# Prompt attention of a two-path decoder step: mask, maxima and inverse sums of a round taken once over four PSUM banks

## The chip, the cores and the metric

The kernel runs on one core of one Trainium2 chip. The metric is the device time of one execution in microseconds (us), lower is better. Three runs of the kernel before took 1689.76, 1691.87 and 1692.32 us, so its median is 1691.87 us.

## The reference, cut to what matters

The whole step is a two-layer decoder trunk (gMLP mixing, attention with three branches, two SwiGLU layers) over 512 prompt tokens and 8 x 4 sample tokens, all in fp32. The change touches only the prompt's attention in two of its branches: the selected blocks (with 8 blocks and a top 16, all of the causal past is selected) and the sliding window of 512 (again all of the causal past). For both, per head and query:

```python
s = einsum(q, k) * HEAD_DIM ** -0.5          # 512 keys at most, 16 heads in 4 groups, head size 64
s = where(mask, s, -inf)                     # causal
m = max(s, axis=-1)                          # of a row; 0 if not finite
e = where(mask, exp(s - m), 0)
p = e / maximum(sum(e), 1e-30)
o = gate_cmp * o_cmp + gate_slc * (p_slc @ v_slc) + gate_win * (p_win @ v_win)
```

## The kernel before, in words

Each engine runs its own program in order; they meet at semaphores. The long stages around the one that is changed are weight products (line 573 and line 601), which take most of the span. The stage of the prompt's attention runs over PAIRS = 32 rounds. Round u takes one query tile of 128 rows (`pair`: tile 3 first, eight rounds for each tile, so rounds 0 to 7 have 512 keys, 8 to 15 have 384, 16 to 23 have 256 and 24 to 31 have 128) and two heads, which lie in partitions 0 to 63 and 64 to 127 of the same query column. A round has two halves v = 2u and 2u + 1: branch 0 (selected) and branch 1 (window). The names of the steps in order:

- TensorE `scores(v)` (line 946): q times k for both heads, into PSUM banks 0 and 1 for branch 0, banks 2 and 3 for branch 1. It waits until the exponentials of the same branch in the round before have read these banks (`a_ex`). Both scores of a round are issued back to back.
- VectorE `maxima(v)` (lines 1986 to 1988): adds the causal mask to the diagonal tile of two banks, takes the row maxima over two banks, and makes the bias of the exponentials; then raises `a_mx`.
- ScalarE `exps(v)` (line 1455): two exponentials with their row sums, PSUM to the SBUF tile PB; raises `a_ex`.
- VectorE `inverse_sums(v)` (lines 1993 and 1994): one over the sums; raises `a_f`.
- GpSimd (line 2123): scales both halves of PB by the inverse sums and the branch's gate.
- TensorE `turn_probs(v)` (line 960): transposes PB into banks 5 to 7, three buffers that rotate over v and head. The second head of half 2u - 1 takes the bank that ScalarE must first have read for half 2u - 2.
- ScalarE (line 1469) and VectorE (line 2002) `probs_turned(v)`: copy the transposes of one head each into PTs.
- TensorE `weigh(v)` (lines 973 and 978): probabilities times values; ScalarE `heads_out` (line 1461) stores the sum of the three branches.

The order in which each engine does these in round u is written out by hand:

- TensorE: scores(2u), scores(2u+1), weigh(2u-4), weigh(2u-3), turn_probs(2u-2), turn_probs(2u-1).
- ScalarE: exps(2u), heads_out(u-2), probs_turned(2u-2), exps(2u+1), probs_turned(2u-1).
- VectorE before: inverse_sums(2u-1), maxima(2u), maxima(2u+1), probs_turned(2u-2), inverse_sums(2u), probs_turned(2u-1).

In round 0 VectorE also does `block_sums(3)` for the compressed branch between the two maxima, which GpSimd and then TensorE's `block_turn` (line 936) need before round 1. The cache rows of the last samples are loaded by a queue that waits for the last weigh of this stage, and the sample stage (line 1015 and on) begins on TensorE behind it.

Of the kernel before, what the change touches and what calls it, by code (L numbers as in the profile page):

```python
# [9 lines left out]
ALU = mybir.AluOpType  # L10
ACT = mybir.ActivationFunctionType
AX = mybir.AxisListType

P = 128
# [19 lines left out]
SCALE = HD ** -0.5  # L34
NEG = -1e30
FLOOR = -1e29
# [12 lines left out]
A_P1 = A_P0 + 2 * ACTB  # L49
# [8 lines left out]
C_BONE, C_CAUS, C_CMP = 0, 128, 256  # L58
# [91 lines left out]
def build_program(nc, x_prompt, x_sample, cache_kv_cmp, cache_kv_slc, state_kv_win, page_table,  # L150
# [9 lines left out]
    def at(name, addr, shape, dt=F32):  # L160
        return nc.alloc_sbuf_tensor_at(name, shape, dt, offset=addr)

    def sem(name):
        return ctx.enter_context(nc.semaphore(name))
# [28 lines left out]
    late = at("late", A_X, [P, C_LATE])  # L193
# [3 lines left out]
    gates = at("gates", A_X + C_LATE * 4 + 768, [P, TT, 3 * NH])  # L197
# [40 lines left out]
    PB = at("PB", A_P0, [P, 4, 2, PAST])  # L238
# [2 lines left out]
    vcz = at("vcz", A_P0 + 16384, [P, NG, R, HD])  # L241
    PTs = [at(f"PTs{j}", a, [P, 2, PAST]) for j, a in enumerate((A_SG, A_P1 + 17408, A_P1 + 29696))]
    PTc = kvtok[:, 0:QT, 0:NG * P]
    hst = at("hst", A_P1 + 34816, [P, 4, 8])
    cstat = at("cstat", A_P1 + 34944, [P, 2, 4, NH])
    PD = at("PD", A_P0, [P, 2 * (PAST + TD) + 32])
    PTd = at("PTd", A_P0 + 4608, [P, 8, P])
# [11 lines left out]
    PS = ctx.enter_context(nc.psum_tensor("PS", [P, 8, 512], F32))  # L259
# [41 lines left out]
    a_s, a_mx, a_ex, a_f, a_p = sem("scores_done"), sem("row_maxima"), sem("exponentials"), sem("inverse_sums"), sem("probs_scaled")  # L301
# [42 lines left out]
    def pair(u):  # L344

        return QT - 1 - u // (NH // 2), u % (NH // 2) // R, u % R

    def head(p, g2, r):
        return (2 * p + g2) * R + r
# [802 lines left out]
    def _(act):  # L1152
# [132 lines left out]
        for t in range(TT):  # L1285
            m = P if t < QT else TD
            act.activation(flat[0:m, t * D:(t + 1) * D], xtok[0:m, t, :], ACT.Square,
                           accum_out=stats[0:m, C_MS + t:C_MS + t + 1]).then_inc(sq_ready, 1)
# [87 lines left out]
        for t in range(TT):  # L1376
            m = P if t < QT else TD
            ins = act.activation(gates[0:m, t, :], PS[0:m, 0, t * 48:t * 48 + 48], ACT.Sigmoid,
                                 scale=stats[0:m, C_RS + t:C_RS + t + 1])
# [68 lines left out]
        def exps(v):  # L1448
            qt, br = pair(v // 2)[0], v % 2
            W = (qt + 1) * P  # L1450
            act.wait_ge(a_mx, v + 1)
            if v >= 4:
                act.wait_ge(a_pt, 2 * v - 6)
            for g2 in range(2):
                act.activation(PB[:, v % 4, g2, 0:W], PS[:, 2 * br + g2, 0:W], ACT.Exp, bias=hst[:, v % 4, 2 + g2:3 + g2],  # L1455
                               scale=SCALE, accum_out=hst[:, v % 4, 4 + g2:5 + g2]).then_inc(a_ex, 1)

        def heads_out(u):
            qt, p, r = pair(u)
# [11 lines left out]
        for u in range(PAIRS + 2):  # L1471
            if u < PAIRS:
                exps(2 * u)
            if u == 0:
                act.wait_ge(s_out, OUTS)
                for j in range(QT):
                    act.wait_ge(b_pt, j + 1)
                    act.activation(PTc[:, QT - 1 - j, :], PS[:, 4 + j, :], ACT.Copy).then_inc(b_pe, 1)
            if u >= 2:
                heads_out(u - 2)  # L1480
            if 1 <= u <= PAIRS:
                probs_turned(2 * u - 2)
            if u < PAIRS:
                exps(2 * u + 1)
            if 1 <= u <= PAIRS:
                probs_turned(2 * u - 1)
            if u == 1:
                fill()
                act.wait_ge(z_q, 1)
            if 3 <= u < 7:  # L1490
                sample_queries(2 * u - 6)
                sample_queries(2 * u - 5)
# [57 lines left out]
    def _(dve):  # L1550
        link = Link(dve, dstep)
# [347 lines left out]
        def block_sums(j):  # L1899
            f = cstat[:, 1, j, :]  # L1900
            dve.wait_ge(b_ex, j + 1)
            link(dve.tensor_reduce(f, ecmp[j][:, :, 0:NCMP], AX.X, ALU.add))
            link(dve.tensor_scalar(f, f, 1e-30, None, ALU.max))
            link(dve.reciprocal(f, f))
            g = gates[:, QT - 1 - j, :].rearrange("p (h b) -> p h b", b=NBR)[:, :, 0]
            dve.tensor_tensor(f, f, g, ALU.mult).then_inc(b_f, 1)
# [38 lines left out]
        def cmp_norm(y):  # L1945
            c = y // 2
            n = 2 * NCMP * CHUNK_N[c]
            k, r = chunk(kcr, y).rearrange("p s a m -> p (s a m)"), krs[:, 0:n]
            dve.wait_ge(n_sum, c + 1)
            dve.tensor_scalar(r, PS[:, 7, 0:n], 1.0 / HD, EPS, ALU.mult, ALU.add).then_inc(n_ms, 1)  # L1950
            dve.wait_ge(c_sq, c + 1)
            link(dve.reciprocal(r, r))
            dve.scalar_tensor_tensor(out=k, in0=k, scalar=knc[:, :], in1=r, op0=ALU.mult, op1=ALU.mult).then_inc(n_done, 1)
# [6 lines left out]
        for y in range(CUNITS):  # L1960
# [16 lines left out]
            cmp_join(y)  # L1977
            if y >= 1 and y % 2 == 1:
                cmp_norm(y - 1)
        def maxima(v):  # L1980
            qt, br = pair(v // 2)[0], v % 2
            st = hst[:, v % 4, :]
            S2 = PS[:, 2 * br:2 * br + 2, :]
            d = S2[:, :, qt * P:qt * P + P]
            dve.wait_ge(a_s, v + 1)
            link(dve.tensor_tensor(d, d, late[:, C_CAUS:C_CAUS + P].unsqueeze(1).to_broadcast([P, 2, P]), ALU.add))
            link(dve.tensor_reduce(st[:, 0:2], S2[:, :, 0:(qt + 1) * P], AX.X, ALU.max))  # L1987
            dve.tensor_scalar(st[:, 2:4], st[:, 0:2], FLOOR, -SCALE, ALU.max, ALU.mult).then_inc(a_mx, 1)

        def inverse_sums(v):  # L1990
            f = hst[:, v % 4, 6:8]
            dve.wait_ge(a_ex, 2 * v + 2)
            link(dve.tensor_scalar(f, hst[:, v % 4, 4:6], 1e-30, None, ALU.max))
            dve.reciprocal(f, f).then_inc(a_f, 1)

        def probs_turned(v):
            u = v // 2
            W = (pair(u)[0] + 1) * P
            dve.wait_ge(a_pt, 2 * v + 2)
            if v >= 3:  # L2000
                dve.wait_ge(a_o, v - 2)
            dve.tensor_copy(PTs[v % 3][:, 1, 0:W], PS[:, 5 + (2 * v + 1) % 3, 0:W]).then_inc(a_ptd, 1)

        for u in range(PAIRS + 1):
            if u >= 1:
                inverse_sums(2 * u - 1)
            if u < PAIRS:
                maxima(2 * u)
                if u == 0:
                    block_sums(QT - 1)  # L2010
                maxima(2 * u + 1)
            if u >= 1:
                probs_turned(2 * u - 2)
            if u < PAIRS:
                inverse_sums(2 * u)
            if u >= 1:
                probs_turned(2 * u - 1)

        W = PAST + TD
# [65 lines left out]
    @block.gpsimd  # L2085
    def _(pool):
        def few_tokens(few, g):
            pool.tensor_tensor(few[:, :, :], hT[:, :, TP:T], gains[:, g:g + KT].unsqueeze(2).to_broadcast([P, KT, TD]),
                               ALU.mult).then_inc(f_ready, 1)

        pool.wait_ge(xn_ready, KT)
        few_tokens(few_v, 0)
        pool.wait_ge(xn_ready, 3 * KT)
        few_tokens(few_k, 32)
        few_tokens(few_q, 8)
        pool.wait_ge(g_d, 1)
        pool.wait_ge(c_ss, 1)
        for j in range(QT):
            pool.memset(ecmp[j][:, :, :], 0.0).then_inc(z_set, 1)
        pool.wait_ge(n_done, 1)  # L2100
        pool.memset(kbd, 0.0).then_inc(b_kd, 1)
        pool.wait_ge(b_kd, 1)
        for p in range(2):
            for g2 in range(2):
                rows = slice(64 * g2, 64 * g2 + 64)
                pool.tensor_copy(kbd[rows, p, 32 * g2:32 * g2 + NCMP], kcr[rows, 0, p, :]).then_inc(b_kd, 1)
        for j in range(QT):
            for n, ready, op, done in ((0, b_mx, ALU.subtract, b_sh), (1, b_f, ALU.mult, b_p)):
                if j == QT - 1 and n == 0:
                    pool.wait_ge(t_eva, (TK + TQ) // 2 + TQ)  # L2110
                    pool.memset(vcz[:, :, :, :], 0.0).then_inc(z_set, 1)
                    pool.wait_ge(c_mm, CUNITS)
                    pool.memset(Qbd[:, :, :, :, :], 0.0).then_inc(z_q, 1)
                e = ecmp[j][:, :, 0:NCMP]
                pool.wait_ge(ready, j + 1)
                pool.tensor_tensor(e, e, cstat[:, n, j, :].unsqueeze(2).to_broadcast([P, NH, NCMP]), op).then_inc(done, 1)
        for v in range(HALVES):
            (qt, p, r), br = pair(v // 2), v % 2
            pool.wait_ge(a_f, v + 1)
            for g2 in range(2):  # L2120
                x = PB[:, v % 4, g2, 0:(qt + 1) * P]
                c = 3 * head(p, g2, r) + 1 + br
                pool.tensor_scalar(x, x, hst[:, v % 4, 6 + g2:7 + g2], gates[:, qt, c:c + 1], ALU.mult, ALU.mult).then_inc(a_p, 1)

    ctx.close()

# [29 lines left out]
```

## Time and profile before

| what | value |
|---|---|
| time of the profiled execution | 1692.25 us |
| its span | 1690.4 us |
| median of three runs | 1691.87 us |
| TensorE matmul busy | 1621.9 us, 96% |
| VectorE busy | 867.5 us, 51% |
| ScalarE busy | 558.1 us, 33% |
| GpSimd busy | 93.0 us, 6% |
| mean granted TensorE clock | 0.987 |
| line 573 in the chain that ended last | 61% |
| line 601 in that chain | 13% |
| lines 960, 973 and 946 (this stage) | 2%, 1% and 1% |

Busy time is the time in which an instruction of the engine runs; idle time before an instruction is put down to what released it. The chain that ended last is followed back from the last instruction to what it waited for. In the timelines, consecutive instructions of one line are merged, with their number behind an x: `x8` of line 946 are the scores of both halves of a round, since each fp32 product runs as two passes.

### The profile page before, as it was taken

How to read it: one execution, taken by the hardware profiler on the slowest of the kernel's cores; microseconds unless marked ns; L12 is line 12 of the kernel's file. 1: busy time of each engine (PE TensorE's matmuls, PEld its weight loads, DVE VectorE, ACT ScalarE, POOL GpSimd, SP SyncE). 2: the span in 40 equal slices, each digit the busy share in tenths (PEclk: the TensorE clock that was granted, in tenths of full speed). 3: DMA queues.
4: the chain of work that ended last, by engine and by line, in shares of the span. 5: the costliest groups of instructions: out<-in, count | busy, mean ns of one | idle time of the engine just before them, and what ended most of it. 6: DMA issues, size and time to landing. Idle time of an engine off the chain costs nothing.

```text
span 1690.4 us, 31723 instructions
## 1 busy us (share of the span) xinstructions
PE 1621.9 (96%) x12994; PEld 1503.0 (89%) x12994; DVE 867.5 (51%) x1417; ACT 558.1 (33%) x965; POOL 93.0 (6%) x154
## 2 busy tenths in 40 slices
PE   8999999999999999999998889988889999999998
PEld 7988999999999999999997547655589999999998
DVE  4227754355444444354185779995456444524433
ACT  6334321232212121144344557664343221212111
POOL 0000000000000000000000034551000000000000
PEclk9998999999999999999999989999999999999999
DMA  4247212323232323122244240004532323232211
GB/s 157 75 164 247 75 57 75 105 87 100 75 94 80 100 75 99 63 87 76 78 143 138 76 143 8 2 2 150 150 96 80 96 79 99 75 100 75 100 57 71
DMA packets 134701, 156.70 MB, mean 93 GB/s; under 512 B 11226, under 2 KB 119058, under 8 KB 134194
## 3 DMA queue, kind: packets, MB, share of 16 engines
q1 hardware_dynamic: 134530, 155.42, 28.9%
q8 instruction: 63, 1.03, 0.3%
q14 instruction: 28, 0.23, 0.0%
q10 hardware_dynamic: 80, 0.02, 0.0%
HBM read 149.58 MB, written 14.16 MB: 97 GB/s over the span
## 4 chain that ended last, share of the span: by engine, by line
PE 90%; DVE 5%; ACT 3%; issue 1%; DMA 1%; POOL 0%; DVEq 0%; POOLq 0%; SPq 0%; ACTq 0%
PE PS L573 61%; PE PS L601 13%; PE PS L960 2%; PE PS L891 2%; PE PS L973 1%; PE PS L946 1%; PE PS L608 1%; PE PS L1062 1%; PE PS L751 1%; ACT PB L1455 1%; PE PS L1028 1%; PE PS L864 1%; DVE hst L1987 1%; PE PS L614 1%; PE PS L1015 1%
## 5 line engine op out<-in xcount | busy, mean ns | idle before, releaser
L573 PE MATMUL PS<-act0h,wh 128*128 128x272 f32 x1664 | 346.1, 289 | 1.6 <-DVE sg L1760 1.6
L573 PE MATMUL PS<-act0l,wh 128*128 128x272 f32 x1664 | 344.6, 288 | 0.0
L573 PE MATMUL PS<-act0h,wl 128*128 128x272 f32 x1664 | 344.5, 288 | 0.0
L1158 ACT ACTIVATE wh<-raw 128x2048 fp32r<-128x2048 f32 x106 | 203.0, 1915 | 407.5 <-PE PS L573 407.5
L1556 DVE TENSOR_TENSOR wl<-raw,wh 128x2048 fp32r<-128x2048 f32 x106 | 243.1, 2293 | 176.3 <-ACT wh L1158 176.3
L573 PEld LDWEIGHTS PS<-act0h,wh 128*128 128x128 f32 x1664 | 260.7, 189 | 2.2 <-issue 1.7
L573 PEld LDWEIGHTS PS<-act0l,wh 128*128 128x128 f32 x1664 | 260.5, 188 | 0.0
L573 PEld LDWEIGHTS PS<-act0h,wl 128*128 128x128 f32 x1664 | 260.4, 188 | 0.0
L1589 DVE TENSOR_TENSOR hT<-PS,hT 128x544 f32 (+1 forms) x72 | 52.1, 724 | 214.5 <-PE PS L573 214.2
L601 PE MATMUL PS<-wh,act0h 128*128 128x256 f32 x448 | 130.0, 290 | 0.0
L601 PE MATMUL PS<-wh,act0l 128*128 128x256 f32 x448 | 126.2, 282 | 0.0
L601 PE MATMUL PS<-wl,act0h 128*128 128x256 f32 x448 | 126.2, 282 | 0.0
L573 PE MATMUL PS<-act1h,wh 128*128 128x272 f32 x576 | 119.1, 288 | 0.0
L573 PE MATMUL PS<-act1l,wh 128*128 128x272 f32 x576 | 119.0, 287 | 0.0
L573 PE MATMUL PS<-act1h,wl 128*128 128x272 f32 x576 | 118.9, 287 | 0.0
L573 PE MATMUL PS<-act2h,wh 128*128 128x272 f32 x512 | 106.8, 290 | 5.9 <-DVE act2l L2072 5.9
L573 PE MATMUL PS<-act2l,wh 128*128 128x272 f32 x512 | 106.3, 289 | 0.0
L573 PE MATMUL PS<-act2h,wl 128*128 128x272 f32 x512 | 106.2, 289 | 0.0
L1604 DVE TENSOR_TENSOR sg<-PS,rsb 128x544 f32<-128x544 f32 x44 | 31.7, 724 | 140.5 <-PE PS L573 140.1
L1227 ACT ACTIVATE sg<-sg 128x544 f32<-128x544 f32 x44 | 28.9, 659 | 204.8 <-DVE sg L1604 204.8
L601 PEld LDWEIGHTS PS<-wh,act0h 128*128 128x128 f32 x448 | 84.7, 189 | 10.8 <-issue 10.7
L573 PEld LDWEIGHTS PS<-act1h,wh 128*128 128x128 f32 x576 | 89.8, 188 | 0.0
(300 smaller groups left out, 2507.2 us busy)
## 6 DMA issues: line engine op xcount, KB each, us to landing
raw<-in_ffn_w_gate SPq DMA_DIRECT2D x44, 512.0 KB
raw<-in_ffn_w_up SPq DMA_DIRECT2D x44, 512.0 KB
raw<-in_a_w_in SPq DMA_DIRECT2D x32, 512.0 KB
raw<-in_ffn_w_down SPq DMA_DIRECT2D x32, 512.0 KB
raw<-in_a_w_out SPq DMA_DIRECT2D x16, 512.0 KB
crows<-in_cache_kv_cmp SPq DMA_DIRECT2D x32, 256.0 KB, 2.8
cache<-in_cache_kv_slc SPq DMA_DIRECT2D x32, 256.0 KB, 5.1
cache<-in_state_kv_win SPq DMA_DIRECT2D x8, 1024.0 KB, 8.1
```

Source lines behind the costliest of these rows:

```text
L573: mm = pe.matmul(PS[:, 4 * ps + 2 * mt + h, 0:HALF], W[:, rs, k, mt * P:mt * P + P], Xp[:, k * T + h * HALF:k * T + h * HALF + HALF], star ...
L601: mm = pe.matmul(PS[:, 4 * ps + t // 2, t % 2 * CW:t % 2 * CW + CW], Xp[:, a:a + P], W[:, rs, k, :], start=(k == 0 and W is wh and Xp is x ...
L608: mm = pe.matmul(PS[c:c + 32, 4 * ps + 2, 0:CW], few[:, k, :], raw[:, rs, k, :], start=(k < 4), stop=(k >= 4))
L614: return pe.matmul(PS[0:TD, 4 * ps + 3, 0:CW], sel[:, :], part[:, rs, :], start=True, stop=True)
L751: pe.matmul(PS[:, 4 + 2 * mt, ch * P:ch * P + P], vt[:, ch, f0:f0 + P], wsT[:, g, :], start=False, stop=(ch == QT - 1))
L891: mm = pe.matmul(PS[:, 4 + y % 2, 0:n], W2[:, y % 2, l, :], x[:, :, l, :], start=(l == 0), stop=(l == 7))
L960: tr = pe.transpose(PS[:, 5 + e % 3, kt * P:kt * P + P], PB[:, v % 4, g2, kt * P:kt * P + P], ident)
L1158: act.activation(wh[:, rs, :, :], raw[:, rs, :, :], ACT.Copy).then_inc(w_hi, 1)
L1227: act.activation(sg[:, mt, :], sg[:, mt, :], ACT.Silu).then_inc(g_act, 1)
L1556: dve.tensor_tensor(wl[:, rs, :, :], raw[:, rs, :, :], wh[:, rs, :, :].bitcast(F32), ALU.subtract).then_inc(w_ready, 1)
L1589: dve.tensor_tensor(h, psum_u(s, mt), h, ALU.add).then_inc(free[s], 1)
L1604: dve.tensor_tensor(halved(sg[:, mt, :]), psum_u(0, mt), halved(rsb[:, :]), ALU.mult).then_inc(free[0], 1)
```

## The change

The three tiny arrays per half (maximum, bias, sum, inverse) become one array per round, indexed by round parity, quantity, and branch and head. `maxima` and `inverse_sums` run once a round. `maxima(u)` waits for the scores of both branches; `inverse_sums(u)` waits for all four exponentials of the round. ScalarE waits for the one `a_mx` of the round ahead of both its halves, and GpSimd for the one `a_f`. VectorE's order in round u becomes maxima(u), probs_turned(2u-2), inverse_sums(u), probs_turned(2u-1). The PSUM banks, TensorE's program and its waits are as before.

```diff
-        def maxima(v):
-            qt, br = pair(v // 2)[0], v % 2
-            st = hst[:, v % 4, :]
-            S2 = PS[:, 2 * br:2 * br + 2, :]
-            d = S2[:, :, qt * P:qt * P + P]
-            dve.wait_ge(a_s, v + 1)
-            link(dve.tensor_tensor(d, d, late[...].to_broadcast([P, 2, P]), ALU.add))
-            link(dve.tensor_reduce(st[:, 0:2], S2[:, :, 0:(qt + 1) * P], AX.X, ALU.max))
-            dve.tensor_scalar(st[:, 2:4], st[:, 0:2], FLOOR, -SCALE, ALU.max, ALU.mult).then_inc(a_mx, 1)
+        def maxima(u):
+            qt = pair(u)[0]
+            st = hst[:, u % 2, :, :]
+            S4 = PS[:, 0:4, :]
+            d = S4[:, :, qt * P:qt * P + P]
+            dve.wait_ge(a_s, 2 * u + 2)
+            link(dve.tensor_tensor(d, d, late[...].to_broadcast([P, 4, P]), ALU.add))
+            link(dve.tensor_reduce(st[:, 0, :], S4[:, :, 0:(qt + 1) * P], AX.X, ALU.max))
+            dve.tensor_scalar(st[:, 1, :], st[:, 0, :], FLOOR, -SCALE, ALU.max, ALU.mult).then_inc(a_mx, 1)
...
-            dve.wait_ge(a_ex, 2 * v + 2)
+            dve.wait_ge(a_ex, 4 * u + 4)
...
         for u in range(PAIRS + 1):
-            if u >= 1:
-                inverse_sums(2 * u - 1)
             if u < PAIRS:
-                maxima(2 * u)
+                maxima(u)
                 if u == 0:
                     block_sums(QT - 1)
-                maxima(2 * u + 1)
             if u >= 1:
                 probs_turned(2 * u - 2)
             if u < PAIRS:
-                inverse_sums(2 * u)
+                inverse_sums(u)
             if u >= 1:
                 probs_turned(2 * u - 1)
...
         def exps(v):
-            act.wait_ge(a_mx, v + 1)
+            act.wait_ge(a_mx, v // 2 + 1)
...
-            pool.wait_ge(a_f, v + 1)
+            pool.wait_ge(a_f, v // 2 + 1)
```

## Rows read from the trace of the kernel before

**Rows 1.** Four stretches: length; PE, PEld, DVE, ACT, POOL busy; granted clock; DMA.
```profile
1019.04:1049.23 30.19, 30.19 (x303) 21.70 (x302) 28.35 (x61) 21.57 (x64) 15.12 (x20) 1.00 0.01 2
1065.46:1090.42 24.96, 24.26 (x242) 16.92 (x243) 23.02 (x61) 16.45 (x56) 12.97 (x21) 1.00 0.01 2
1103.51:1120.13 16.62, 14.65 (x147) 10.05 (x146) 15.15 (x48) 10.60 (x45) 8.68 (x17) 1.00 0.01 1
1131.24:1144.54 13.30, 9.89 (x99) 6.85 (x98) 11.86 (x48) 8.04 (x45) 6.97 (x16) 1.00 0.01 2
```

**Rows 2.** Instruction groups of VectorE by line and shape, this stage.
```profile
L1986 DVE TENSOR_TENSOR PS<-PS,late 128x256 f32<-128x256 f32 x64 | 26.8, 419 | 0.1
L1987 DVE TENSOR_REDUCE hst<-PS 128x2 f32<-128x1024 f32 x16 | 19.6, 1224 | 0.5
...
L2002 DVE COPY PTs<-PS 128x512 f32<-128x512 f32 x16 | 11.1, 691 | 2.1 <-PE PS L960 1.5
...
L1987 DVE TENSOR_REDUCE hst<-PS 128x2 f32<-128x256 f32 x16 | 6.8, 424 | 0.5
```

**Rows 3.** Timeline of rounds with 512 keys: start, us, engine, line.
```profile
1018.97 1.99 PE L946 MATMUL PS<-KTb,qTr 64*128 64x512 f32 x8
...
1022.32 0.69 ACT L1455 ACTIVATE PB<-PS,hst 128x512 f32<-128x512 f32 x1 [2.16 <-DVE hst L1988]
...
1025.06 1.13 PE L946 MATMUL PS<-KTb,qTr 64*128 64x512 f32 x4
```

**Rows 4.** Timeline of a round with 384 keys.
```profile
1083.01 0.58 ACT L1455 ACTIVATE PB<-PS,hst 128x384 f32<-128x384 f32 x1 [1.72 <-DVE hst L1988]
...
1085.32 1.56 PE L946 MATMUL PS<-KTb,qTr 64*128 64x384 f32 x8
```

**Rows 5.** Timeline of a round with 256 keys.
```profile
1118.18 0.48 ACT L1455 ACTIVATE PB<-PS,hst 128x256 f32<-128x256 f32 x1 [1.50 <-DVE hst L1988]
...
1120.07 1.25 PE L946 MATMUL PS<-KTb,qTr 64*128 64x256 f32 x8
```

**Rows 6.** Timeline of a round with 128 keys.
```profile
1139.69 0.37 ACT L1455 ACTIVATE PB<-PS,hst 128x128 f32<-128x128 f32 x1 [1.32 <-DVE hst L1988]
...
1141.15 0.93 PE L946 MATMUL PS<-KTb,qTr 64*128 64x128 f32 x8
...
1141.57 0.17 DVE L1993 TENSOR_SCALAR hst<-hst 128x2 f32<-128x2 f32 x1
```

**Rows 7.** Timeline of round 1.
```profile
1007.36 1.13 PE L946 MATMUL PS<-KTb,qTr 64*128 64x512 f32 x4 [0.45 <-ACT PB L1455]
...
1009.34 0.17 DVE L1988 TENSOR_SCALAR hst<-hst 128x2 f32<-128x2 f32 x1
...
1009.54 0.69 ACT L1455 ACTIVATE PB<-PS,hst 128x512 f32<-128x512 f32 x1 [2.23 <-DVE hst L1988]
```

**Rows 8.** Timeline of the end of the stage.
```profile
1147.80 0.93 PE L946 MATMUL PS<-KTb,qTr 64*128 64x128 f32 x8
...
1151.20 1.74 POOL L2123 TENSOR_SCALAR PB<-PB,hst,gates 128x128 f32<-128x128 f32 x4 [1.58 <-DVE hst L1994]
...
1155.14 4.37 PE L1015 MATMUL PS<-cst,cache 128*128 128x128 f32 x32
```

**Rows 9.** Timeline of TensorE: two gaps, and scores near the lower clock.
```profile
966.83 1.97 PE L877 MATMUL PS<-kvtok,qTn 128*128 128x64 f32 x8 [3.52 <-DVE kvtok L1950]
...
983.64 0.62 PE L919 MATMUL PS<-cst,kvtok 128*31 128x128 f32 x4 [2.27 <-ACT vc L1410]
...
1005.27 1.64 PE L946 MATMUL PS<-KTb,qTr 64*128 64x512 f32 x4
```

**Rows 10.** Short stretches of TensorE around those gaps: busy, granted clock.
```profile
965.20:965.60 0.40, 0.00 (x0) 0.73 0.00 0
...
982.00:984.00 2.00, 0.36 (x4) 1.00 0.00 0
...
1005.20:1005.60 0.40, 0.40 (x3) 0.50 0.94 328
```

More of the change, by code:

```diff
@@ L243, in build_program @@
     PTc = kvtok[:, 0:QT, 0:NG * P]
-    hst = at("hst", A_P1 + 34816, [P, 4, 8])
+    hst = at("hst", A_P1 + 34816, [P, 2, 4, 4])
     cstat = at("cstat", A_P1 + 34944, [P, 2, 4, NH])
@@ L1450, in exps @@
             W = (qt + 1) * P
-            act.wait_ge(a_mx, v + 1)
+            st = hst[:, v // 2 % 2, :, :]
+            act.wait_ge(a_mx, v // 2 + 1)
             if v >= 4:
@@ L1454, in exps @@
             for g2 in range(2):
-                act.activation(PB[:, v % 4, g2, 0:W], PS[:, 2 * br + g2, 0:W], ACT.Exp, bias=hst[:, v % 4, 2 + g2:3 + g2],
-                               scale=SCALE, accum_out=hst[:, v % 4, 4 + g2:5 + g2]).then_inc(a_ex, 1)
+                act.activation(PB[:, v % 4, g2, 0:W], PS[:, 2 * br + g2, 0:W], ACT.Exp,
+                               bias=st[:, 1, 2 * br + g2:2 * br + g2 + 1], scale=SCALE,
+                               accum_out=st[:, 2, 2 * br + g2:2 * br + g2 + 1]).then_inc(a_ex, 1)
         def heads_out(u):
@@ L1979, in _, with inverse_sums @@
                 cmp_norm(y - 1)
-        def maxima(v):
-            qt, br = pair(v // 2)[0], v % 2
-            st = hst[:, v % 4, :]
-            S2 = PS[:, 2 * br:2 * br + 2, :]
-            d = S2[:, :, qt * P:qt * P + P]
-            dve.wait_ge(a_s, v + 1)
-            link(dve.tensor_tensor(d, d, late[:, C_CAUS:C_CAUS + P].unsqueeze(1).to_broadcast([P, 2, P]), ALU.add))
-            link(dve.tensor_reduce(st[:, 0:2], S2[:, :, 0:(qt + 1) * P], AX.X, ALU.max))
-            dve.tensor_scalar(st[:, 2:4], st[:, 0:2], FLOOR, -SCALE, ALU.max, ALU.mult).then_inc(a_mx, 1)
-        def inverse_sums(v):
-            f = hst[:, v % 4, 6:8]
-            dve.wait_ge(a_ex, 2 * v + 2)
-            link(dve.tensor_scalar(f, hst[:, v % 4, 4:6], 1e-30, None, ALU.max))
-            dve.reciprocal(f, f).then_inc(a_f, 1)
+        def maxima(u):
[4 more added lines that the diff above has]
+            dve.wait_ge(a_s, 2 * u + 2)
+            link(dve.tensor_tensor(d, d, late[:, C_CAUS:C_CAUS + P].unsqueeze(1).to_broadcast([P, 4, P]), ALU.add))
+            link(dve.tensor_reduce(st[:, 0, :], S4[:, :, 0:(qt + 1) * P], AX.X, ALU.max))
+            dve.tensor_scalar(st[:, 1, :], st[:, 0, :], FLOOR, -SCALE, ALU.max, ALU.mult).then_inc(a_mx, 1)
+        def inverse_sums(u):
+            st = hst[:, u % 2, :, :]
+            dve.wait_ge(a_ex, 4 * u + 4)
+            link(dve.tensor_scalar(st[:, 3, :], st[:, 2, :], 1e-30, None, ALU.max))
+            dve.reciprocal(st[:, 3, :], st[:, 3, :]).then_inc(a_f, 1)
         def probs_turned(v):
@@ L2122, in _ @@
                 c = 3 * head(p, g2, r) + 1 + br
-                pool.tensor_scalar(x, x, hst[:, v % 4, 6 + g2:7 + g2], gates[:, qt, c:c + 1], ALU.mult, ALU.mult).then_inc(a_p, 1)
+                pool.tensor_scalar(x, x, hst[:, v // 2 % 2, 3, 2 * br + g2:2 * br + g2 + 1], gates[:, qt, c:c + 1], ALU.mult, ALU.mult).then_inc(a_p, 1)
     ctx.close()
```

## The prediction

> **What bounds the kernel now.** I read the page first: over the span TensorE is busy 96% and the weight products dominate, so this change can only matter inside its own stage, from 994 to 1155 us, and by what it does to TensorE's way through it, because the sample stage's first transposes follow the last weigh directly and the cache loads of the last samples also wait for that weigh. Then I read the stage in windows of whole rounds. The first stretch holds five rounds, the second five, the third and fourth four each, so a round takes 30.19/5 = 6.04 us with 512 keys, 24.96/5 = 4.99 with 384, 16.62/4 = 4.16 with 256 and 13.30/4 = 3.33 with 128. TensorE is busy 6.04, 4.85, 3.66 and 2.47 us of these, VectorE 5.67, 4.60, 3.79 and 2.97 [rows 1]. So with 512 keys TensorE itself is the bound; with 384 VectorE and the hand-overs between engines share it, and below that neither is full. ScalarE is busy 4.3 us or less of a round, but it is idle in one piece: 2.16, 1.72, 1.50 and 1.32 us in front of the first exponential of a round, waiting for the bias from VectorE [rows 3 to 6]. That idle piece tells how the rounds are chained: the score banks are single, so scores of the next round wait for this round's exponentials, which wait for its maxima.
>
> **What the change removes and adds.** VectorE's instructions in this stage fall from 64 to 32 in each of five kinds (mask, maximum, bias, floor of the sums, inverse). A reduce over 256 elements takes 0.424 us and one over 1024 takes 1.224 [rows 2]: 1.042 ns an element and a fixed 0.157. Hence one over 2048 is 0.157 + 2.134 = 2.29 us, over 1536 1.76, over 1024 1.22 (measured), over 512 0.69. The mask over 256 elements takes 0.419; for 512 the nearest row is a copy of 512 elements out of PSUM, 0.691 [rows 2], and I take 0.69; the bounds are 0.42 (width costs nothing) and 0.84 (two of the old ones). For the reduce over 2048 the bounds are 1.22 and 2.45. The tiny operations stay near 0.17. So VectorE works less per round: 0.5 to 0.6 us.
>
> But the first exponential of a round now waits for both branches. Before, maxima(2u) ran beside scores(2u+1) and maxima(2u+1) ran beside exps(2u); these two overlaps are what goes. GpSimd's scaling of the first half also starts only after all four exponentials, and VectorE's last copy of a round lies behind the same wait.
>
> **The loop that then sets a round.** I start at the moment when both scores of a round are complete. (a) VectorE: mask 0.69 + 0.04 to the next, maximum (by keys) + 0.03, bias 0.17 + 0.04 to ScalarE. The hand-over of the bias takes 1009.54 - 1009.34 = 0.20 us from its start [rows 7]; I use 0.21. That is 3.26, 2.73, 2.19 and 1.66 us for 512, 384, 256 and 128 keys. (b) From the first exponential to the next round's scores: ScalarE does exps(2u), heads_out and its copy of half 2u-2, which frees the bank for TensorE's last transposes of half 2u-1, and the scores stand behind these in TensorE's order. This piece is unchanged and I read it whole: 1025.06 - 1022.32 = 2.74 [rows 3], 1085.32 - 1083.01 = 2.31 [rows 4], 1120.07 - 1118.18 = 1.89 [rows 5], 1141.15 - 1139.69 = 1.46 us [rows 6]. (c) Both scores: 1.99, 1.56, 1.25, 0.93 [rows 3 to 6], + 0.05 to VectorE. Sums: **8.04, 6.65, 5.38 and 4.10 us a round, against 6.04, 4.99, 4.16 and 3.33**: +2.00, +1.66, +1.22, +0.77.
>
> Is anything else late in this loop? GpSimd starts some 0.6 us before the scores are complete (the exponentials end about 1.1 us ahead of that at 512 keys), needs 15.12/5 = 3.0 us for a round at most [rows 1], and is done before TensorE needs the second half, since the weighs stand in between. VectorE's last copy lies behind exps(2u+1) and the inverse: this way round closes within 0.3 us of the loop above at 512 keys and about equals it at 128 keys, so it adds nothing but a few hundredths. ScalarE's small extra work (sample queries, the zero-padded values) falls into its new idle time. The other cost of GpSimd, that VectorE's tiny operations were sometimes stretched beside it, goes.
>
> **The sum.** Round 0 and 1: block_sums comes after one long maxima instead of a short one, so TensorE's block_turn and with it scores(3) come between 0 and 1.3 us later; I take 0.5. Scores(3) then end at 1007.36 + 1.13 + 0.5 = 1009.0 [rows 7], the scores of round 2 start at 1009.0 + 3.26 + 2.74 = 1015.0, those of round 3 at 1023.1 instead of 1018.97 [rows 3]: +4.1. Rounds 3 to 30: 5 x 8.04 + 8 x 6.65 + 8 x 5.38 + 7 x 4.10 = 165.1 us, against 1147.80 - 1018.97 = 128.8 [rows 3, 8]: +36.3. The end: before, 1155.14 - 1147.80 = 7.34 us pass from the last scores to the sample stage [rows 8]. After: scores 0.98, VectorE 1.66, to the inverse 1141.57 - 1139.69 = 1.88 [rows 6], inverse and hand-over 0.45, GpSimd 1.74, and the 2.20 us that remain behind GpSimd's end at 1152.94 [rows 8]: 8.9, +1.6. Together **+42 us**. Behind the stage nothing gives it back, as TensorE and the loads both hang on its end.
>
> **TensorE's clock.** In this stage it was granted 1.00 throughout the four stretches, that is 2.4 GHz [rows 1]. After the change TensorE idles 8.04 - 6.04 = 2.0 us a round at 512 keys, in one piece ahead of the last transposes (1.8, 1.7 and 1.6 us for the others, there in part before). In the trace an idle gap of 3.52 us lost the clock about 2 us in, a gap of 2.27 us did not [rows 9, 10]. So gaps of 2.0 us are at the edge. At 1.2 GHz the loop pays for its scores and last transposes: the four score passes took 1.64 us with the clock at 0.50 for part of them, against 1.13 [rows 7, 9, 10], so both scores cost 1.0 us more at least, and at most double, 2.0; with the transposes I take 2.0 us for a round that is hit at 512 keys, 1.5, 1.0 and 0.5 for the others. I reckon with three rounds of eight at 512 keys: **+6 us**. The Trainium skill, TensorE: Matmul & The Clock Gate, Part 1, says that the low clock is the default and that sustained activity lifts it, and its section on HAM oscillation describes kernels that lose it again in each turn of a loop. By that rule every round would be hit, which is the second rival below; the trace, with one gap that kept the clock and one that lost it, does not decide.
>
> Forecast: span 1690.4 + 48 = 1738, execution 1692.25 + 48 = 1740 us. The profiled execution lies 0.4 us above the median, so the median becomes 1740.
>
> **The rivals.**
> 1. *VectorE was the bound, and gains.* If VectorE's throughput set the rounds and the exponentials' later start fell wholly into ScalarE's idle piece, a round would fall by VectorE's saved 0.5 us in the 24 rounds below 512 keys, 12 us in all: 1680. For it: VectorE is the busiest engine at 384 keys and below in part (4.60 of 4.99, 3.79 of 4.16) [rows 1]. Against it: the idle piece is 2.16 us or less [rows 3 to 6], the new start is later by more, and the banks are single. It decides where the exponentials start less than that piece later, which holds nowhere by my sum. 2%. The Trainium skill, VectorE: DVE Perf Modes, in the section on the TRN2 errata, has a fixed cost for each instruction and advises fewer, larger ones; the fixed 0.157 us of the reduce agrees, and this rule speaks for the rival.
> 2. *The clock is lost in nearly every round.* Then 8 x (2.0 + 1.5 + 1.0 + 0.5) = 40 us come on top of 42: 1774; if in half of them, 1754. For it: the new gap of each round; against it: the 2.27 us gap that held [rows 9, 10]. 13%.
> 3. *Width is cheap.* If an operation over four banks costs near the lower bounds (mask 0.42, the reduce some 0.4 under my line), each round is 0.7 us shorter: 32 x 0.7 = 22 us less, 1718. Against it: the reduce's time is linear in its elements from 256 to 1024 [rows 2]. 8%.
> 4. *The change is hidden or worth nothing* (within 0.2%): only if the mask and maxima of both branches already waited for each other in VectorE, which the start of the first exponential ahead of the second mask's end denies. 1%.
>
> **How the numbers follow.** The forecast's case, the loop with the clock lost in none to about half of the rounds, has 76% and its own range of 1728 to 1756. The range, with part of rivals 2 and 3 and the bounds of the mask (0.42 to 0.84, some 8 us up or down less 4), is 1726 to 1764. What a measurement of this kernel can tell from no change is about 0.2%, 3.4 us. Faster 2%, same 1%, slower 97%.
>
> **What would show it.** Right: rounds of 8.0, 6.7, 5.4 and 4.1 us; the first exponential 3.3 us after the scores at 512 keys; a mask of 0.69 and a reduce of 2.29 us; TensorE idle ahead of line 960 for ScalarE's copy; the chain through the lines of mask, maximum, exponential, copy and scores, and no longer through line 973. Wrong: rounds of 6 us at 512 keys, or ScalarE's first exponential starting less than 2 us after the scores; a granted clock well under 1 in this stage would put rival 2 in its place.

## The result and the profile after

The changed kernel takes 1743.42 us (median of four runs, 1738.61 to 1744.91) against 1692.09 us for the kernel before beside it: a ratio of 1.0299, 95% interval 1.0283 to 1.0314, slower. Beside later kernels it took 1742.29 (ratio 1.0305, 1.0288 to 1.0322). Forecast were 1740 and a range of 1726 to 1764. The profiled execution took 1744.82 us, its span is 1743.0.

The instructions of VectorE that answer to [rows 2], by line and shape (count, busy us, mean ns, idle before). There are 32 of each kind now (the maxima in four shapes of eight), and the times of the maxima lie on the line drawn through the old shapes:

```profile
L1988 DVE TENSOR_TENSOR PS<-PS,late 128x512 f32<-128x512 f32 x32 | 22.4, 699 | 12.9 <-PE PS L946 11.8
L1989 DVE TENSOR_REDUCE hst<-PS 128x4 f32<-128x2048 f32 x8 | 18.3, 2291 | 0.3
L1989 DVE TENSOR_REDUCE hst<-PS 128x4 f32<-128x1536 f32 x8 | 14.1, 1757 | 0.3
L1989 DVE TENSOR_REDUCE hst<-PS 128x4 f32<-128x1024 f32 x8 | 9.8, 1225 | 0.3
...
L1989 DVE TENSOR_REDUCE hst<-PS 128x4 f32<-128x512 f32 x8 | 5.5, 691 | 0.3
```

A round with 512 keys, from its scores to the next ones (timeline of the changed kernel, to be held against [rows 3]):

```profile
1023.70 1.99 PE L946 MATMUL PS<-KTb,qTr 64*128 64x512 f32 x8
...
1025.73 0.70 DVE L1988 TENSOR_TENSOR PS<-PS,late 128x512 f32<-128x512 f32 x1
1026.47 2.29 DVE L1989 TENSOR_REDUCE hst<-PS 128x4 f32<-128x2048 f32 x1
...
1028.80 0.17 DVE L1990 TENSOR_SCALAR hst<-hst 128x4 f32<-128x4 f32 x1
...
1029.00 0.69 ACT L1456 ACTIVATE PB<-PS,hst 128x512 f32<-128x512 f32 x1 [4.12 <-DVE hst L1990]
...
1030.34 0.27 ACT L1463 ACTIVATE oT<-PS 128x128 f32<-128x128 f32 x1
1030.49 0.60 ACT L1471 ACTIVATE PTs<-PS 128x512 f32<-128x512 f32 x1
...
1031.15 0.66 PE L960 MATMUL PS<-cst,PB 128*128 128x128 f32 x4 [1.89 <-ACT PTs L1471]
...
1031.74 3.28 PE L946 MATMUL PS<-KTb,qTr 64*128 64x512 f32 x8
```

From mask to first exponential it is 1029.00 - 1025.73 = 3.27 us (forecast 3.26), from there to the next scores 2.74 us, as before. From scores to scores it is 1031.74 - 1023.70 = 8.04 us. ScalarE's idle piece grew from 2.16 to 4.12 us, and TensorE now waits 1.89 us for ScalarE's copy. The last line also shows the other part of the loss: the same eight score passes took 3.28 us instead of 1.99. A later round shows when this happens, first in TensorE's timeline and then in short stretches (length, TensorE busy, granted clock, DMA):

```profile
1048.52 0.66 PE L960 MATMUL PS<-cst,PB 128*128 128x128 f32 x4 [1.89 <-ACT PTs L1471]
1049.10 3.57 PE L946 MATMUL PS<-KTb,qTr 64*128 64x512 f32 x8
```

```profile
1047.20:1048.00 0.80, 0.00 (x0) 1.00 0.00 0
1048.00:1048.80 0.80, 0.28 (x3) 1.00 0.05 10
1048.80:1049.60 0.80, 0.80 (x6) 0.85 0.00 0
1049.60:1050.40 0.80, 0.80 (x4) 0.50 0.00 0
1050.40:1051.20 0.80, 0.80 (x4) 0.50 0.00 0
1051.20:1052.00 0.80, 0.80 (x4) 0.50 0.00 0
1052.00:1052.80 0.80, 0.80 (x4) 0.52 0.00 0
1052.80:1053.60 0.80, 0.80 (x18) 1.00 0.00 0
```

TensorE waits until 1048.52 for the copy, and soon after it starts again the clock is at 0.50 of full, which is 1.2 GHz, for more than 3 us, just while the scores run that the loop waits for. That round took 1052.71 - 1043.10 = 9.61 us from mask to mask; the one ahead of it, whose scores all ran at the full clock, 8.04.

What waited for whom between 1020 and 1200 us (total us, times, longest). The kernel before had 72.0 and 47.8 us in the first two of these lines between 1008 and 1155 us, and none of VectorE's waits there came to more than 5.4 us in total:

```profile
POOL PB L2122 <- DVE hst L1996: 112.7, 29, 6.6
ACT PB L1456 <- DVE hst L1990: 91.2, 29, 5.2
DVE hst L1995 <- ACT PB L1456: 60.8, 29, 2.9
PEld PS L960 <- ACT PTs L1471: 44.5, 29, 2.1
```

VectorE has less to do and waits more. Where the 52.6 us between the two spans lie: the stage, from the first scores to the sample stage's first transposes, took 1155.14 - 994.38 = 160.8 us before and 1206.07 - 992.89 = 213.2 after, +52.4. The work ahead of it was 1.5 us shorter, the sample stage 1.1 and the rest 0.5 us longer; such pieces differ by that much between profiles. I use this stage length for all kernels below.

### The profile page after: what moved, and what is told of

It is laid out like the page before. It is cut to its first block and busy times, and to the rows that moved or that the text cites. A ratio compares the mean times of both kernels' runs of the same rounds, so it can differ in the third digit from the quotient of the medians.

```text
span 1743.0 us, 31563 instructions
## 1 busy us (share of the span) xinstructions
PE 1640.5 (94%) x12994; PEld 1508.5 (87%) x12994; DVE 844.8 (48%) x1257; ACT 557.1 (32%) x965; POOL 92.6 (5%) x154
## 5 line engine op out<-in xcount | busy, mean ns | idle before, releaser
L1456 ACT ACTIVATE PB<-PS,hst 128x512 f32<-128x512 f32 (+3 forms) x128 | 66.8, 535 | 101.4 <-DVE hst L1990 97.7
L960 PE MATMUL PS<-cst,PB 128*128 128x128 f32 x320 | 53.2, 292 | 45.1 <-ACT PTs L1471 41.5
```

What stands on the lines that cost most here:

```text
L960: tr = pe.transpose(PS[:, 5 + e % 3, kt * P:kt * P + P], PB[:, v % 4, g2, kt * P:kt * P + P], ident)
```

## Experiments

**The wait alone.** In the kernel before, the first half's maxima wait for both scores.

```diff
-            dve.wait_ge(a_s, v + 1)
+            dve.wait_ge(a_s, v // 2 * 2 + 2)
```

> The kernel before with one wait changed: maxima(2u) waits for the scores of both branches, as in the change; all operations stay over two banks. Theory (the loop: scores, maxima, exponentials, copy, scores): from both scores to the first exponential it takes 1.93, 1.67, 1.40 and 1.13 us for 512, 384, 256 and 128 keys, a round 6.7, 5.6, 4.6 and 3.6 us against 6.04, 4.99, 4.16 and 3.33: +15 us, 1707, with the granted clock at 1.00. Rival 1 (the wider operations alone cost the time): +0 to 2 us. Rival 2 (the clock makes most of the 51 us of the change): near +0, since TensorE's gap grows by 0.7 us only.

Measured: 1703.17 us, ratio 1.0074 (1.0057 to 1.0091); stage 172.7 us, +11.9. Rounds from mask to mask with 512, 384, 256 and 128 keys: 6.70, 5.59, 4.58 and 3.56 us. The loop gives 6.71, 5.59, 4.59 and 3.57. The sum is 3 us short of +15, mostly because I had charged all 32 rounds in full: the first three rounds and the end of the stage together cost 0.2 us (round 2 takes 6.86 us in both kernels), and in the first rounds after each change of the number of keys the kernel before, too, is slower than its usual round (5.76, 5.22 and 5.21 us at 384 keys). The clock stayed at 1.00 from 1008 us on. Both rivals fall: with not one operation changed and the clock held, waiting alone costs 12 us.

**The mask merged.**

```diff
-            d = S2[:, :, qt * P:qt * P + P]
-            dve.wait_ge(a_s, v + 1)
-            link(dve.tensor_tensor(d, d, late[...].to_broadcast([P, 2, P]), ALU.add))
+            if br == 0:
+                d = PS[:, 0:4, qt * P:qt * P + P]
+                dve.wait_ge(a_s, v + 2)
+                link(dve.tensor_tensor(d, d, late[...].to_broadcast([P, 4, P]), ALU.add))
             link(dve.tensor_reduce(st[:, 0:2], S2[:, :, 0:(qt + 1) * P], AX.X, ALU.max))
```

> The kernel before with the mask alone merged: one mask over four banks after both scores, then maxima and bias by halves as before. Theory (the loop): 2.19, 1.93, 1.66 and 1.39 us to the first exponential, rounds of 6.97, 5.85, 4.85 and 3.83 us, +24 us, 1716. Each step of the ladder (wait +15, mask +9, maximum +21) is the time by which the first exponential starts later. Rival 1 (number of instructions counts): 32 masks fewer should give back some 5 us against the kernel that only waits. Rival 2 (clock): no step between the two.

Measured: 1716.1 us, ratio 1.0149 (1.0132 to 1.0166); stage 184.1 us, +23.3. Rounds: 6.97, 5.85, 4.84 and 3.83 us. This has 32 masks fewer on VectorE than the run above and is 13 us slower (11.4 in the two stages). Of the 11.4 us, 8.2 lie in rounds 3 to 30, where each round is longer by the 0.27 us by which the first bias comes later; 2.4 lie in the first rounds, where round 1 took 8.45 us instead of 6.54 with the clock partly down (0.65 between 1010 and 1013 us), and the rest at the end. Two rounds with 128 keys took 4.27 us, with the clock at 0.50 from 1156 to 1164 us. The step from this kernel to the changed one is 29.1 us of stage: its rounds are longer by 1.07, 0.80, 0.53 and 0.33 us, some 22 us, and the clock costs most of the rest.

**Inverse sums by halves, maxima merged.** The changed kernel, with `inverse_sums(v)` again for each half.

```diff
...
         for u in range(PAIRS + 1):
+            if u >= 1:
+                inverse_sums(2 * u - 1)
             if u < PAIRS:
                 maxima(u)
...
-                inverse_sums(u)
+                inverse_sums(2 * u)
...
-            pool.wait_ge(a_f, v // 2 + 1)
+            pool.wait_ge(a_f, v + 1)
```

> The changed kernel with inverse sums by halves again, in the places of the kernel before; mask and maxima stay merged. Theory (the loop through the maxima sets the round): rounds stay at 8.04, 6.65, 5.38 and 4.1 us plus what the clock adds, the end is about 1 us shorter because GpSimd starts on the first half sooner: 1742, within 2 us of the changed kernel. Rival (GpSimd's late start on the first half is a good part of the loss): 10 us or more come back, 1733 or less.

Measured: 1744.77 us, ratio 1.0312 (1.0295 to 1.0329); stage 215.4 us. Nothing comes back, and the rival (GpSimd's late start) falls: in the changed kernel the merged inverses cost nothing that these runs can tell from the clock, only 0.05 us a round with 128 keys (4.10 here, 4.15 there). The 1 us at the end does not show: from the last mask to the sample stage it is 7.70 us, against 8.06 and 8.15 in the two profiles of the changed kernel.

**Inverse sums merged, maxima by halves.**

```diff
...
+            h = hst[:, 2 * (u % 2):2 * (u % 2) + 2, :]
+            f = h[:, :, 6:8]
+            dve.wait_ge(a_ex, 4 * u + 4)
+            link(dve.tensor_scalar(f, h[:, :, 4:6], 1e-30, None, ALU.max))
...
-            if u >= 1:
-                inverse_sums(2 * u - 1)
...
-                inverse_sums(2 * u)
+                inverse_sums(u)
...
-            pool.wait_ge(a_f, v + 1)
+            pool.wait_ge(a_f, v // 2 + 1)
```

> The kernel before with inverse sums merged alone, in the change's place (ahead of VectorE's copy of half 2u-1), mask and maxima by halves as before. Theory: alone it makes a loop of its own, because VectorE's copy and with it the next mask now stand behind exps(2u+1): first exponential to inverse 3.44, 2.94, 2.41 and 1.88 us, inverse, copy, mask, maximum and bias behind it, rounds of 6.5, 5.5, 4.5 and 3.6 us, +12 us, 1704. This loss is covered in the changed kernel by the longer loop of the maxima. Rival (fewer instructions on VectorE, and GpSimd has slack): 32 pairs of small operations fewer bring up to 0.35 us in the rounds with 384 keys, 1689 to 1692.

Measured: 1701.42 us, ratio 1.0064 (1.0047 to 1.008); stage 169.6 us, +8.8. Rounds: 6.28, 5.42, 4.56 and 3.48 us. So this half of the change would have cost on its own; behind the longer loop of the maxima it is hidden. Two losses of one change do not add.

**Was it the place or the merging?** The same, with VectorE's copy of half 2u-1 ahead of the merged inverses (the edit is shown against the kernel of the run above).

```diff
-            if u < PAIRS:
-                inverse_sums(u)
             if u >= 1:
                 probs_turned(2 * u - 1)
+            if u < PAIRS:
+                inverse_sums(u)
```

> The kernel before with the inverse sums merged, as in the run of that kind, but behind VectorE's copy of half 2u-1 instead of ahead of it; mask and maxima by halves. Theory (it was the place ahead of the copy that cost the 10 us, not the merging): that loss goes, 1691 to 1694. Rival (GpSimd's start on the first half, which is still as late as in that run, cost it): it stays, 1701.

Measured: 1694.85 us, ratio 1.0016 (1.0007 to 1.0026), just above the 1691 to 1694 expected; stage 161.8 us, +1.0. Rounds: 6.28, 4.96, 4.08 and 3.29 us, so below 512 keys the whole loss is gone and the rounds are even 0.03 to 0.07 us shorter than before. It was the place. At 512 keys the 6.28 us stay, for another reason, which the timeline shows:

```profile
1025.86 3.02 POOL L2122 TENSOR_SCALAR PB<-PB,hst,gates 128x512 f32<-128x512 f32 x4 [3.27 <-DVE hst L1995]
...
1027.55 0.60 DVE L1988 TENSOR_SCALAR hst<-hst 128x2 f32<-128x2 f32 x1
...
1028.18 0.69 ACT L1455 ACTIVATE PB<-PS,hst 128x512 f32<-128x512 f32 x1 [1.86 <-DVE hst L1988]
```

The bias of two elements a row takes 0.60 us instead of 0.17. It ends where GpSimd's third operation ends (1025.86 + 3 x 0.76 = 1028.14). The kernel before has the same thing at another point of GpSimd's four operations:

```profile
1019.24 3.02 POOL L2123 TENSOR_SCALAR PB<-PB,hst,gates 128x512 f32<-128x512 f32 x4 [3.95 <-DVE hst L1994]
...
1020.07 0.17 DVE L1994 RECIPROCAL hst<-hst 128x2 f32<-128x2 f32 x1
...
1021.88 0.41 DVE L1988 TENSOR_SCALAR hst<-hst 128x2 f32<-128x2 f32 x1
```

The bias ends at 1022.29, with GpSimd's fourth operation (1022.26). In that stage 36 of the 38 tiny TENSOR_SCALARs of VectorE that took over 0.2 us beside GpSimd ended within 0.05 us behind the end of one of its operations; the 31 reciprocals of the same size that began inside one all took 0.17. The Trainium skill, SBUF — State Buffer, in its section "SBUF: two separate sides", describes a port pair that VectorE and GpSimd share as an exclusive lock, held for a whole instruction, when VectorE's operation runs in a two-port mode or has two SBUF inputs. The rows agree with a lock; no run here shows in which mode the bias runs.

The stretch accounts for the round. Without it the way from scores to scores is 1.18 + 1.73 + 0.21 + 2.74 = 5.86 us (to the first mask, to the bias, to the exponential, to the next scores); with the 0.43 us of stretch that is 6.29, measured 6.28. In the kernel before the stretch was 0.24 and 0.12 us in turns, which makes 6.10 and 5.98, measured 6.09 and 5.97.

The profiled execution is 1.9 us longer than that of the kernel before: 1.0 in the stage and 1.2 right behind it, where the sample stage's first 36 passes took 5.55 us at a clock of 0.66 instead of 4.36 at 0.84. The two medians lie 3.5 us apart; only the profiled execution can be taken apart like this.

**ScalarE's copy out of the loop.** The changed kernel, with another order on ScalarE.

```diff
         for u in range(PAIRS + 2):
+            if u >= 2:
+                heads_out(u - 2)
+            if 1 <= u <= PAIRS:
+                probs_turned(2 * u - 2)
             if u < PAIRS:
                 exps(2 * u)
...
-            if u >= 2:
-                heads_out(u - 2)
-            if 1 <= u <= PAIRS:
-                probs_turned(2 * u - 2)
             if u < PAIRS:
                 exps(2 * u + 1)
```

> The changed kernel with ScalarE's order turned: heads_out and its copy of half 2u-2 run ahead of exps(2u), in the time in which ScalarE waits for the bias. Theory (the loop runs through that copy and TensorE's last transposes): the copy leaves the loop, which now is maxima, four exponentials in a row, the second scores: 7.3, 5.95, 4.9 and 3.9 us a round instead of 8.04, 6.65, 5.38 and 4.1: -17 us, and up to 8 us more where the shorter gaps of TensorE keep the clock: 1718 to 1726. Rival (VectorE's order or GpSimd closes a loop as long): 1738 to 1743.

Measured: 1724.91 us, ratio 1.0194 (1.0177 to 1.0211) against the kernel before, 17.4 us under the changed kernel beside it; stage 192.8 us. Rounds: 7.33, 6.10, 4.93 and 3.80 us. The rival falls, and the loop is shown to run through ScalarE's copy and TensorE's last transposes.

**The clock.** The changed kernel, with the transposes of one head issued four times.

```diff
+                for again in range(4 if e % 4 == 2 else 1):
                     for kt in range(qt + 1):
                         tr = pe.transpose(...)
```

> The changed kernel with TensorE's gap filled: the transposes of the first head of half 2u-1 are issued four times instead of once (the same values to the same places, 1.5 us more work at 512 keys, 1.1, 0.75 and 0.4 us for the others, in a gap of 2.0 to 1.6 us). Theory (8 of the 51 us are a clock lost in the gaps, and what TensorE does there counts for it whatever it is): granted clock near 1.00 in the stage and rounds of 8.04 us without the longer ones, 1733 to 1737. Rival (transposes do not hold the clock, or the extra work is late): 1743 or more.

Measured: 1738.15 us, ratio 1.0271 (1.0253 to 1.0288), 4.1 us under the changed kernel beside it (1742.29) and 1 us above the 1733 to 1737 expected; stage 207.0 us against 213.2 and 212.0 in its two profiles. Stretches of this kernel (length, TensorE busy, clock):

```profile
1023.70:1055.90 32.20, 29.88 (x291) 1.00 0.01 2
1068.00:1108.00 40.00, 36.34 (x361) 1.00 0.00 1
1120.00:1150.00 30.00, 25.95 (x253) 1.00 0.01 2
1165.00:1190.00 25.00, 19.45 (x176) 1.00 0.00 1
```

From round 3 on the rounds take their 8.04, 6.65, 5.37 or 4.16 us, but for the first after each change of the number of keys. More work on TensorE makes the kernel faster. It does not win all of the clock's cost back: round 1 still took 9.07 us, as the scores at its end ran partly at 0.50, and between 1195 and 1200 us, behind the last round, the clock was at 0.63.

The same with ordinary products in the gap:

```diff
+                if e % 4 == 2:
+                    for again in range(3):
+                        for kt in range(qt + 1):
+                            pe.matmul(PS[:, 5 + e % 3, kt * P:kt * P + P], ident, PB[:, v % 4, g2, kt * P:kt * P + P],
+                                      start=True, stop=True)
```

> As the kernel before it in this list, but the gap is filled with ordinary fp32 products into the same PSUM places, which the transposes then overwrite: three sets, each two passes, so up to 3 us at 512 keys, more than the gap there holds, and 2.2, 1.5 and 0.75 us for the others. Theory (activity of any kind holds the clock): clock near 1.00, but at 512 keys about 1 us a round too much work, 1737 to 1745. If the transposes leave the clock as it is and this one lifts it, the kind of work counts.

Measured: 1742.61 us, ratio 1.0307 (1.029 to 1.0324). The clock is 1.00 in all four stretches read between 1008 and 1200 us, but the rounds at 512 keys take 8.61 us, since the extra work does not fit the gap. Gain and cost cancel. From round 3 to the last, transposes hold the clock as products do. In round 1 only this one of the two held it (7.87 us against 9.07), but its extra work is also longer, so the kind of work is not shown to be the reason.

**A version faster than both.** The kernel before, with two operations taken off the loop, and one of the two alone.

```diff
-            link(dve.tensor_scalar(f, hst[:, v % 4, 4:6], 1e-30, None, ALU.max))
-            dve.reciprocal(f, f).then_inc(a_f, 1)
+            dve.reciprocal(f, hst[:, v % 4, 4:6]).then_inc(a_f, 1)
...
-            if u >= 2:
-                heads_out(u - 2)
             if 1 <= u <= PAIRS:
                 probs_turned(2 * u - 2)
             if u < PAIRS:
                 exps(2 * u + 1)
             if 1 <= u <= PAIRS:
                 probs_turned(2 * u - 1)
+            if u >= 2:
+                heads_out(u - 2)
```

> The kernel before with two operations taken off the loop: ScalarE stores heads_out at the end of its round (where it is idle) and not between exps(2u) and its copy of half 2u-2, and the sums are inverted without the floor of 1e-30 (a row's own largest term adds 1 to its sum, so the floor never acts). Theory: with 512 keys TensorE is the bound and nothing changes; below, heads_out leaves 0.16 us a round where ScalarE is on the loop and the floor 0.2 us where VectorE is: -6 to -9 us, 1683 to 1686. Rival (another hand-over, GpSimd's or the weighs', is as late): -2 us or less.

> The kernel before with only the move of heads_out to the end of ScalarE's round. Theory: 0.16 us in each of the 24 rounds below 512 keys, -3 to -4 us, 1688. Rival: 0, if VectorE's part of the loop is as long.

Measured: both edits 1687.29 us, ratio 0.9975 (0.9965 to 0.9986), stage 155.6 us (-5.2), rounds of 5.97, 4.82, 3.94 and 3.12 us; the move of heads_out alone 1691.22 us, ratio 0.9999 (0.999 to 1.0008), stage 159.5, rounds of 5.96, 4.97, 4.15 and 3.32 us. Both forecasts were misses: the move alone gave 0.1 us and not 3 to 4, as its rival said, and the two edits gave 4.0 and not 6 to 9. Below 512 keys the move alone shortens no round and both together shorten one by 0.17 to 0.21 us. The floor alone was not run, so whether the move adds anything is not shown. 1687 is the fastest kernel here, 0.25% under the one before.

## Why the prediction was right

Point by point:

- *The operations.* Mask 0.699 us (0.69), reduces 2.291, 1.757 and 1.225 us (2.29, 1.76, 1.22), bias to ScalarE 0.20 (0.21). Right. Rival 3 (width is cheap) falls. The bounds of the mask, 0.42 and 0.84 us, are worth 9 us down and 5 us up over 32 rounds; the prediction's "8 us up or down less 4" does not say that clearly.
- *The loop.* 8.04, 6.65, 5.38 and 4.10 us were forecast. With the clock held the rounds take 8.04, 6.65, 5.37 and 4.16 us, and from the scores of round 3 to those of round 31 it is 166.4 us in the kernel with repeated transposes, against 165.1 in the sum. The wait alone and the wait with the mask moved the rounds by what the loop says to 0.02 us, the order on ScalarE to 0.15. With 128 keys the round closes through VectorE's last copy, 0.05 us later, as the prediction had left open.
- *Nothing is given back behind the stage.* Right: +52.4 us in the stage, +52.6 in the span.
- *The clock.* Forecast +6 us, in three rounds of eight at 512 keys. In rounds 3 to 30 the changed kernel took, from mask to mask, 172.3 us where the kernel with repeated transposes took 165.4: +6.9 (+5.6 in its second profile). The total was right, in part by luck: a hit costs less than forecast and there are more of them. At 512 keys four of the rounds 1 to 7 were hit, by 1.0 to 1.6 us and not 2.0, and single ones at 384 (8.29), 256 (6.06, 5.89) and 128 keys (4.58), where none had been reckoned with. At 512 keys the same four rounds are hit in both profiles of the kernel (1, 3, 5 and 6); below, other ones. Rival 2 (each turn of the loop loses the clock) does not hold: most rounds kept it over the same gap. The prediction also read the Trainium skill too widely there: in its page TensorE: Matmul & The Clock Gate, the section on HAM oscillation has an example with longer waits in each turn of the loop than these gaps.
- *The sizes that were off.* The stage's 52.4 us are 4.4 above the forecast 48. Of these, 2.1 lie ahead of the scores of round 3 (30.81 us behind the first scores; forecast 28.7). Half of that is round 1's scores, which end 15.72 us behind the first scores and not 14.11 + 0.5:

```profile
1004.52 4.09 PE L946 MATMUL PS<-KTb,qTr 64*128 64x512 f32 x8
...
1013.91 0.66 PE L960 MATMUL PS<-cst,PB 128*128 128x128 f32 x4 [3.11 <-ACT PTs L1471]
1014.50 3.11 PE L946 MATMUL PS<-KTb,qTr 64*128 64x512 f32 x8
```

  They begin 0.74 us later than before and take 4.09 us, at a clock of 0.50 nearly throughout, where the kernel before had 1.00 for the second half of them; so this too is in good part the clock. The other half is the next scores, 3.11 us instead of 1.99. A further 1.3 us are the loop itself (166.4 against 165.1), most of it in the first round after each change of the number of keys (6.98, 5.87 and 4.49 us), 0.9 the clock in rounds 3 to 30, and 0.1 the end (9.04 us against 8.9).
- *Rival 1* (VectorE's throughput) falls: VectorE's busy time over the span went from 867.5 to 844.8 us, 0.71 a round, and the kernel lost 51 us. The prediction's own rows give 0.8 us a round, not the 0.5 to 0.6 it states. Its test of this rival was also wrong. By its own sum the first exponential comes 2.00, 1.66, 1.22 and 0.77 us later, which is less than the idle pieces of 2.16, 1.72, 1.50 and 1.32 us everywhere, not nowhere. The idle piece does not take up the delay, because the next scores wait for these exponentials: it grew to 4.12 us.
- *Two readings that did not hold.* At 512 keys TensorE was not the only bound before: the loop through the maxima, with GpSimd's stretch, gives that kernel's 6.09 and 5.97 us, while the two kernels of the last experiment go down to 5.96. And the sign "no longer through line 973" did not show everywhere. In rounds with 384 keys the chain of the profile still goes through lines 973 and 960 to ScalarE at 1079.51 us. But the first exponential there had begun at 1079.03, released by the bias, and the rounds are the loop's 6.65 us.

## What to carry to other kernels

Merging instructions pays on an engine that is full; where the work goes round a loop over several engines with single buffers, the first result's time is what counts, and a merge moves it to that of the last. Before merging, sum the loop once as it would then be, from one piece to the same piece of the next round, out of the trace; here that gave the rounds of six kernels to within 0.25 us where the clock held (the change, the wait, the mask, the two with the inverse sums, the order on ScalarE), but not those of the last experiment, where the move alone shortened nothing. A loop that gets longer can cost twice: the gaps it opens on TensorE can take its clock, and the loss then falls on the very products that the loop waits for.

## What the runs showed of the hardware that I had not expected

- The clock does not fall in every gap of the same kind. Over gaps of about 2 us on TensorE (1.89 in the row at 1048.52) it was held in most rounds and fell in some, below 512 keys at other rounds in the two profiles of one kernel. In the round shown it was back after some 3 us; in the kernel with the mask merged it stayed at 0.50 from 1156 to 1164 us. From round 3 on, repeated transposes held it as well as products.
- An operation of VectorE on 2 elements a row took up to 0.60 us instead of 0.17 and ended with GpSimd's running operation; reciprocals of the same size were not held up. With GpSimd's start moved within the round, the rounds at 512 keys took 6.28 us instead of about 6.0.
